# Channel statistics of a layer norm moved from TensorE to VectorE, in a hybrid decoder step on one Trainium2 core

## The reference, cut to what matters

```python
def conformer_layer(x, conv_prev, g_pre, w_in, conv_w, conv_b, ln_g, ln_b, w_out, g_post):
    h = rms_norm(x, g_pre)
    a, b, z = jnp.split(h @ w_in, 3, axis=-1)
    glu = a * jax.nn.sigmoid(b)
    full = jnp.concatenate([conv_prev, glu], axis=1)
    c = depthwise_conv(full, conv_w) + conv_b              # 31 taps
    y = jax.nn.silu(layer_norm(c, ln_g, ln_b)) * jax.nn.silu(z)
    return x + rms_norm(y @ w_out, g_post), full[:, -(CONV_W - 1):]

def layer_norm(x, g, b):
    mu = jnp.mean(x, axis=-1)                              # over 1024 channels
    var = jnp.mean(jnp.square(x - mu), axis=-1)
    return (x - mu) * lax.rsqrt(var + EPS) * g + b

def compress(rows, pe, w1, w2):                            # once for k, once for v
    # rows in chunks of 16, two chunks beside each other, against w1 (2048 x 256)
    return jax.nn.silu(pre) @ w2
```

## Time and profile before

| | |
|---|---|
| median of 3 runs | 974.96 us (973.85 to 976.8) |
| profiled execution, its own time | 973.55 us |
| its span | 971.4 us |
| PE busy | 908.4 us, 94% of the span |
| DVE, ACT, POOL busy | 530.2, 437.2, 301.2 us |

### The profile page before, as it was taken

How to read it: one execution, slowest core, us unless ns; L and a number is a source line. 1 busy time by engine, 2 the same in 40 slices (tenths; PEclk the granted TensorE clock), 3 DMA queues, 4 the chain that set the end, 5 groups by cost and what they waited for, 6 DMA issues and landing times.

```text
span 971.4 us, 16757 instructions
## 1 busy us (share of the span) xinstructions
PE 908.4 (94%) x6278; PEld 771.1 (79%) x6278; DVE 530.2 (55%) x1173; ACT 437.2 (45%) x895; POOL 301.2 (31%) x311
## 2 busy tenths in 40 slices
PE   2799999998999999999979999999999999799995
PEld 2699999954369877878979898989898988686663
DVE  2477999983861664331234555545454545535563
ACT  4356767632511533232344555455464545423421
POOL 1269888870670000003003322323232333400000
PEclk9999999999999999999979999999999999999997
DMA  7345433147618124265222222223132100922521
GB/s 215 84 111 174 119 89 96 58 111 255 220 41 296 44 82 133 49 141 155 68 70 62 66 45 66 51 60 88 36 75 44 45 1 25 271 88 82 182 78 33
DMA packets 156071, 97.43 MB, mean 100 GB/s; under 512 B 97156, under 2 KB 144932, under 8 KB 155911
## 3 DMA queue, kind: packets, MB, share of 16 engines
q1 hardware_dynamic: 141134, 77.07, 29.8%
q0 software_dynamic: 4896, 10.32, 3.1%
q10 hardware_dynamic: 9961, 8.97, 2.8%
HBM read 87.48 MB, written 18.85 MB: 109 GB/s over the span
## 4 chain that ended last, share of the span: by engine, by line
PE 84%; SPq 4%; DVE 3%; ACT 3%; DMA 3%; issue 2%; ACTq 0%; POOL 0%; DVEq 0%
PE psum L1741 9%; PE psum L2056 7%; PE psum L1760 6%; PE psum L1761 6%; PE psum L1762 6%; PE psum L2057 6%; PE psum L2058 6%; PE psum L2151 5%; PE psum L2121 4%; PE psum L2086 4%; PE psum L2104 3%; PE psum L1976 3%; PE psum L1975 3%; PE psum L1977 3%; PE psum L1833 3%; SPq L551 2%
## 5 line engine op out<-in xcount | busy, mean ns | idle before, releaser
L2056 PE MATMUL psum<-u_hi,tile_hi 128*128 128x288 f32 x464 | 147.2, 317 | 8.6 <-ACT arena L761 8.4
L761 ACT ACTIVATE arena<-psum 128x512 f32<-128x512 f32 (+9 forms) x214 | 82.1, 433 | 148.4 <-PE psum L1977 48.8
L740 POOL TENSOR_SCALAR arena<-arena,kept 128x512 f32<-128x512 f32 (+3 forms) x128 | 82.7, 661 | 184.0 <-DVE kept L1607 184.0
L2057 PE MATMUL psum<-u_lo,tile_hi 128*128 128x288 f32 x464 | 138.5, 299 | 0.0
L2058 PE MATMUL psum<-u_hi,tile_lo 128*128 128x288 f32 x464 | 137.5, 296 | 0.0
L1316 DVE SCALAR_TENSOR_TENSOR psum<-arena,psum 128x512 f32<-128x512 f32 x168 | 127.0, 756 | 6.0
L1760 PE MATMUL psum<-h_hi,tile_hi 128*128 128x288 f32 x384 | 115.2, 300 | 4.1 <-DVE tile_lo L1288 4.1
L1761 PE MATMUL psum<-h_lo,tile_hi 128*128 128x288 f32 x384 | 114.7, 299 | 0.0
L1762 PE MATMUL psum<-h_hi,tile_lo 128*128 128x288 f32 x384 | 114.3, 298 | 0.0
L2056 PEld LDWEIGHTS psum<-u_hi,tile_hi 128*128 128x128 f32 x464 | 88.3, 190 | 20.3 <-ACT arena L761 12.2
L1538 DVE COPY arena<-psum 128x512 f32<-128x512 f32 (+3 forms) x72 | 37.0, 513 | 103.8 <-PE psum L2104 101.0
(11 more groups left out here) (285 smaller groups left out, 1781.9 us busy)
## 6 DMA issues: line engine op xcount, KB each, us to landing
tile_whole<-in_b_w_in SPq DMA_DIRECT2D x64, 256.0 KB
tile_whole<-in_a_w_in SPq DMA_DIRECT2D x24, 512.0 KB
arena<-in_cmp_w SPq DMA_DIRECT2D x3, 2048.0 KB, 10.3
kvw_whole<-in_w_kv SPq DMA_DIRECT2D x6, 1024.0 KB, 11.5
bias_copies<-bias_line POOLq DMA_DIRECT2D x4, 1280.0 KB, 24.3
arena<-in_x_prompt SPq DMA_DIRECT2D x8, 512.0 KB, 10.0
arena<-in_a_w_out SPq DMA_DIRECT2D x4, 1024.0 KB, 16.8
arena<-bias_copies SPq DMA_DIRECT2D x16, 256.0 KB, 3.7
```

Of the source, the lines that this page charges most:

```text
L740: pool.tensor_scalar(L, L, rden[:, stat(n) + k:stat(n) + k + 1], gR[:, i, h:h + 1], ALU.mult, ALU.mult).then_inc(S["pn_ready"], 1)
L761: return nc.scalar.activation(out, in_, ACT.Copy, scale=scale)
L2056: pe.matmul(pb(7, HT), w_hi, u_hi[:, k, here], start=(k == 0), stop=False)
L2057: pe.matmul(pb(7, HT), w_hi, u_lo[:, k, here], start=False, stop=False)
```

## The change

The channel sums of the mean become seven adds on DVE into `chan_sum`, and one matmul of it. The squares are summed by seven adds on DVE into `square_slot(0)` (four slots in place of two, so that ACT may run ahead), and their one matmul stands between the two halves of `compress(1)`. The transposes for `conv_prompt` come ahead of `compress(0)`. The values' compression weights go into a place of their own, `w1_far`, over the prompt's GLU rows, issued ahead of chunks 25 to 27; the later reload of `w1_sb` with the same weights (needed by the prompt's compression) and `gpost_a` come behind `compress(1)`. POOL's two DRAM-to-DRAM copies come behind the bias tables. DVE's sample sums are spread anew: 0 and 1 ahead of the mean, 2 behind the copies, 3 to 6 behind the adds of squares, 7 to 9 behind the scaling, 10 to 15 last.

```diff
+        def square_slot(m):
+            i = m if m < 4 else (1, 2, 3, 1)[m - 4]
+            return sg[:, i, 0:SEQ] if i < 2 else square_far[:, i % 2]
+        SUMS = CONV * KD + KD - 1
...
@@ sync, c == C_OA, behind past_cmp(12..15)
-                if c == C_KV - 1:
-                    sp.wait_ge(S["cs_mm"], 2)
-                    sp.dma_start(w1_sb, I["cmp_w1"][1]...).then_inc(S["w1_in"], 16)
                     sp.wait_ge(S["conv_step"], CONV * KD)
                     sp.wait_ge(S["co_tr"], 1)
-                    sp.dma_start(gpost_a, ...).then_inc(S["gpost_in"], 16)
+                    sp.dma_start(w1_far, I["cmp_w1"][1]...).then_inc(S["w1_in"], 16)
+                if c == C_KV - 1:
                     for t in range(4):
...
+                    sp.wait_ge(S["stat_mm"], 1 + KD)
                     sp.dma_start(x_sb[0:NS, 4], ...).then_inc(x_in[4], 16)
+                    sp.wait_ge(S["cs_mm"], 5)
+                    sp.dma_start(gpost_a, ...).then_inc(S["gpost_in"], 16)
+                    sp.dma_start(w1_sb, I["cmp_w1"][1]...).then_inc(S["w1_in"], 16)
                     sp.wait_ge(S["sample_sums"], 2 * KD)
@@ gpsimd: L687 and L688 moved from ahead of the sample products to behind L704
@@ scalar
-                if m >= 2:
-                    act.wait_ge(S["stat_mm"], m)
-                nc.scalar.activation(sg[:, m % 2, 0:SEQ], conv[:, m, 0:SEQ], ACT.Square)
+                if m >= 4:
+                    act.wait_ge(S["conv_step"], SUMS + m - 3)
+                nc.scalar.activation(square_slot(m), conv[:, m, 0:SEQ], ACT.Square)
@@ vector
+            for m in range(1, KD):
+                dve.wait_ge(S["conv_step"], CONV * KD + m - 1)
+                V.tensor_tensor(out=chan_sum, in0=chan_sum if m > 1 else conv[:, 0, 0:SEQ], in1=conv[:, m, 0:SEQ],
+                                op=ALU.add).then_inc(S["conv_step"], 1)
+            for n in range(2):
+                sample_sum(n)
             dve.wait_ge(S["stat_mm"], 1)
...
-            for n in range(4):
+            sample_sum(2)
+            for m in range(1, KD):
+                dve.wait_ge(S["sqd"], m + 1)
+                if m > 1:
+                    dve.wait_ge(S["conv_step"], SUMS + m - 1)
+                V.tensor_tensor(out=square_slot(0), in0=square_slot(0), in1=square_slot(m), op=ALU.add)...
+            for n in range(3, 7):
                 sample_sum(n)
@@ tensor
                 for ht in range(2):
+                    if c and ht:
+                        pe.wait_ge(S["conv_step"], SUMS + KD - 1)
+                        pe.matmul(pb(1, SEQ), ones, square_slot(0), ...).then_inc(S["stat_mm"], KD)
...
-            for m in range(KD - 2):
-                mean_part(m)
-            compress(0)
-            mean_part(KD - 2)
-            mean_part(KD - 1).then_inc(S["stat_mm"], 1)
             (transposes for conv_prompt, co_tr)
+            compress(0)
+            pe.wait_ge(S["conv_step"], SUMS)
+            pe.matmul(pb(0, SEQ), ones, chan_sum, ...).then_inc(S["stat_mm"], 1)
...
-            for m in range(KD):
-                pe.wait_ge(S["sqd"], m + 1)
-                pe.matmul(pb(1, SEQ), ones, sg[:, m % 2, 0:SEQ], ...).then_inc(S["stat_mm"], 1)
             compress(1)
```

More of the change, by code:

```diff
@@ L135, in build @@
         tap_sum = at(R_X + KD * NT, SEQ)
+        chan_sum = at(R_X + KD * NT, SEQ)
+        square_far = at(R_X + 4 * D, 2, SEQ)
         last_rows_in = at(R_X + 2 * D, 4, KV, P)
@@ L167, in build @@
         w1_sb = at(R_G + 4224, 16, 256)
+        w1_far = at(R_F, 16, 256)
         rows_ring = at(R_G + 8320, 2, KV, P)
@@ L572, in _ @@
                         past_cmp(n)
-                if c == C_KV - 1:
-                    sp.wait_ge(S["cs_mm"], 2)
-                    sp.dma_start(w1_sb, I["cmp_w1"][1].rearrange("(j p) n -> p j n", p=P)).then_inc(S["w1_in"], 16)
                     sp.wait_ge(S["conv_step"], CONV * KD)
                     sp.wait_ge(S["co_tr"], 1)
-                    sp.dma_start(gpost_a, I["a_norm_post"][0:1, :].broadcast_to([P, D])).then_inc(S["gpost_in"], 16)
+                    sp.dma_start(w1_far, I["cmp_w1"][1].rearrange("(j p) n -> p j n", p=P)).then_inc(S["w1_in"], 16)
+                if c == C_KV - 1:
                     for t in range(4):
@@ L582, in _ @@
                         sp.dma_start(x_sb[:, t], I["x_prompt"][0, t * P:(t + 1) * P, :]).then_inc(x_in[t], 16)
+                    sp.wait_ge(S["stat_mm"], 1 + KD)
                     sp.dma_start(x_sb[0:NS, 4], I["x_sample"].rearrange("b t d -> (b t) d")).then_inc(x_in[4], 16)
+                    sp.wait_ge(S["cs_mm"], 5)
+                    sp.dma_start(gpost_a, I["a_norm_post"][0:1, :].broadcast_to([P, D])).then_inc(S["gpost_in"], 16)
+                    sp.dma_start(w1_sb, I["cmp_w1"][1].rearrange("(j p) n -> p j n", p=P)).then_inc(S["w1_in"], 16)
                     sp.wait_ge(S["sample_sums"], 2 * KD)
@@ L685, in _ @@
                     split_lo_a(3 * m + 7)
-            pool.dma_start(O["conv_sample"][0, :, 0:W - 1 - DS, :], I["state_conv"][0, :, DS:W - 1, :]).then_inc(S["late"], 16)
-            pool.dma_start(O["win_sample"][:, 0:PAST], I["state_win"]).then_inc(S["late"], 16)
             pool.wait_ge(S["state_ready"], 16)
@@ L704, in _ @@
                 pool.dma_start(bias_copies[h0:h0 + 4], bias_dram[h0:h0 + 4].unsqueeze(1).broadcast_to([4, P, NX])).then_inc(S["bias_out"], 16)
+            pool.dma_start(O["conv_sample"][0, :, 0:W - 1 - DS, :], I["state_conv"][0, :, DS:W - 1, :]).then_inc(S["late"], 16)
+            pool.dma_start(O["win_sample"][:, 0:PAST], I["state_win"]).then_inc(S["late"], 16)
             pool.wait_ge(S["x1_out"], 16 * TT)
@@ L904, in _ @@
                 act.wait_ge(S["centred"], m + 1)
-                if m >= 2:
-                    act.wait_ge(S["stat_mm"], m)
-                nc.scalar.activation(sg[:, m % 2, 0:SEQ], conv[:, m, 0:SEQ], ACT.Square).then_inc(S["sqd"], 1)
+                if m >= 4:
+                    act.wait_ge(S["conv_step"], SUMS + m - 3)
+                nc.scalar.activation(square_slot(m), conv[:, m, 0:SEQ], ACT.Square).then_inc(S["sqd"], 1)
             act.wait_ge(S["co_tr"], 1)
@@ L1326, in sample_sum @@
                                 ALU.add).then_inc(S["sample_sums"], 1)
+            for m in range(1, KD):
[4 more added lines that the diff above has]
+                sample_sum(n)
             dve.wait_ge(S["stat_mm"], 1)
             for m in range(KD):
-                dve.wait_ge(S["conv_step"], CONV * (m + 1))
                 V.tensor_tensor(out=conv[:, m, 0:SEQ], in0=conv[:, m, 0:SEQ], in1=pb(0, SEQ), op=ALU.subtract).then_inc(S["centred"], 1)
@@ L1335, in _ @@
                               pb(ct_bank(DB + b), KV, 16, 8)).then_inc(S["ct_ready"], 1)
-            for n in range(4):
+            sample_sum(2)
[3 more added lines that the diff above has]
+                    dve.wait_ge(S["conv_step"], SUMS + m - 1)
+                V.tensor_tensor(out=square_slot(0), in0=square_slot(0), in1=square_slot(m), op=ALU.add).then_inc(S["conv_step"], 1)
+            for n in range(3, 7):
                 sample_sum(n)
@@ L1345, in _ @@
                 V.tensor_tensor(out=conv[:, m, 0:SEQ], in0=conv[:, m, 0:SEQ], in1=rstd_ln[:, 0:SEQ], op=ALU.mult).then_inc(S["lnx_ready"], 1)
-            for n in range(4, 7):
+            for n in range(7, 10):
                 sample_sum(n)
@@ L1354, in _ @@
                 V.tensor_copy(new_rows[:, :, DS * b:DS * b + DS], glu_s[:, :, b, W - 1:W - 1 + DS]).then_inc(S["new_packed"], 1)
-            for n in range(7, 2 * KD):
+            for n in range(10, 2 * KD):
                 sample_sum(n)
@@ L1831, in compress @@
                 for ht in range(2):
+                    if c and ht:
+                        pe.wait_ge(S["conv_step"], SUMS + KD - 1)
+                        pe.matmul(pb(1, SEQ), ones, square_slot(0), start=True, stop=True).then_inc(S["stat_mm"], KD)
                     for j in range(16):
-                        ins = pe.matmul(pb(cs_bank(c, ht), 33, NCS), w1_sb[:, j, ht * P:(ht + 1) * P],
+                        ins = pe.matmul(pb(cs_bank(c, ht), 33, NCS), (w1_far if c else w1_sb)[:, j, ht * P:(ht + 1) * P],
                                         ctS[:, j % 8, :, j // 8:j // 8 + NCS], start=(j == 0), stop=(j == 15))
@@ L1864, in _ @@
             pe.wait_ge(S["glu_ready"], 3 * KD)
-            def mean_part(m):
-                pe.wait_ge(S["conv_step"], CONV * (m + 1))
-                return pe.matmul(pb(0, SEQ), ones, conv[:, m, 0:SEQ], start=(m == 0), stop=(m == KD - 1))
-            for m in range(KD - 2):
-                mean_part(m)
-            compress(0)
-            mean_part(KD - 2)
-            mean_part(KD - 1).then_inc(S["stat_mm"], 1)
             pe.wait_ge(S["sg_ready"], KD)
@@ L1878, in _ @@
             ins.then_inc(S["co_tr"], 1)
+            compress(0)
+            pe.wait_ge(S["conv_step"], SUMS)
```

(6 more changed lines are left out.)

## The result

The changed kernel takes 966.04 us (median of 4 runs, 965.39 to 968.51) against 975.62 us (4 runs) of the kernel before: ratio 0.9908, 95% interval 0.9884 to 0.9932, that is 6.6 to 11.3 us faster. Six more runs on another occasion gave 968.07 us (964.74 to 968.67), ratio 0.9924 (0.9904 to 0.9943). I had forecast 968.7, in a range of 965 to 972.5. The profiled execution took 965.92 us with a span of 964.0; against 973.55 and 971.4 that is 7.6 and 7.4 us less, where the sum said 6.3.

What follows compares the result with a forecast made beforehand. PE was taken to bound the kernel (84% of the chain), with DVE's chain then setting its restart: -8.8 us plus 2.5 us for the clock gives -6.3, from 974.96 to 968.7 us, range 965 to 972.5.

Steps and rivals of the forecast that it cites:

- the sum: Whole kernel: -8.8 us from leg 2 plus 2.5 us for the clock, together -6.3 us.
- Leg 1: PE up to compress(1): compress(0) starts at 198.25, compress(1) at 236.5 in place of 250.95, 14.5 us earlier, weights in time.
- Leg 2: DVE's chain from sum of squares to packed rows: PE idles 4.7 us, transposes start at 273.6 for 282.36, -8.8 us.
- The clock: Row products after PE's idle before the new rows' transposes: slow restart at half clock, 2.5 to 4.1 us, 2.5 taken.
- POOL against the adds: DVE beside POOL's products: L1351 kept at 8.8 us; about 2 us per blocked add could hit the new adds.
- rival 3: POOL blocks DVE's adds before eps, so DVE's chain starts 2.6 us later: 971.3 us, up to 972.9; chance 0.15.
- Moved transfers: Loads and copies issued later: gpost_a covered by 11 us, key/value weights landed at 307 before ACT reads at 332.
- case 1: The main forecast, with two clock prices and 1 us either way of DVE's chain: 967.0 to 971.3 us; chance 0.5.
- Rival 5: Queues fill with moved copies and bias tables, key/value weights land at 341, ACT 9 us late: 978 us; chance 0.05.

Runs made afterwards that it cites:

- sums-later run: Sample sums 7 to 9 moved behind the packing of the new rows, against the changed kernel: 959.86 us, ratio 0.9851 to the kernel before.
- the four corners with the squares: Changed kernel, squares on DVE or PE, sums 7 to 9 in place or behind packing: DVE 966.04 and 959.86 us, PE 965.00 and 964.56.
- the fill: Five extra 512-column matmuls, results unused, in PE's idle stretch before the new rows' transposes, against the changed kernel: 965.56 us.
- weights_late: Changed kernel, but w1_far loaded behind the output projection's weights and the first compression, copies still moved: 966.69 us, ratio 0.9917 to the kernel before.

## Why the prediction was right, point by point

- **Leg 1, PE up to the second compression: right.** 198.23 and 236.87 came out where 198.25 and 236.5 were said, with no wait for weights.
- **Leg 2, DVE's chain sets the restart: right, and shown** by the sums-later run and by the four corners with the squares. Transposes at 273.83 for 273.6, an idle of 4.65 for 4.7. What the prediction didn't draw from it is that with this chain the squares' move buys nothing.
- **The clock: right in kind, too dear.** I took 2.5 us from the two later restarts; the fill shows 1.4. The slow stretch ran from the restart at 273.83 to before 277, shorter than the 4.9 us of the earlier trace rows from which the term came. That is 1.1 of the 1.3 us by which the sum fell short of the profiled execution. The medians' further 2 us lie within their spread, in which the sparse transposes' clock has a part.
- **POOL against the adds:** the conflict is there, smaller than rival 3 had it. The squares' adds took 7.22 for 5.1 (product 5 over their start), and DVE still idled 1.80 before eps. The channel adds too took 5.91 for 5.1, with POOL's first products over their start, and were covered. L1372 stayed at 8.79 as said, and fell to 4.90 without POOL.
- **"Moved transfers": the step that failed**, though the total doesn't show it. I treated the copies' move only as a risk for what comes later, and held the early weights for safe "with POOL's copies still in the queues", 6.4 us early. The runs say the reverse: with the copies moved the weights' order matters nothing (weights_late), and the copies' place is worth 5.6 to 7.7 us, through loads that I had not looked at, the last cached rows. Beside the copies the weights would have landed at 240.7 and not at 230.1. That the forecast held is luck in this respect: the change moved the copies, so the loads landed in 3.0 us at most, and the weights in 8.4. The row that would have told it was in the trace before, 22.7 us at most against a median of 2.5.
- **A slip in the range.** With a clock price of 2.5 us at least and 1 us either way, case 1 begins at 967.7 and not at 967.0; nothing hangs on it.
- **Rival 5 (late key/value weights): absent.** Issued at 282.62, they landed in 23.2 us by the median of the two; the copies took 43.7 and nobody waited for them.

So the gain was an interplay. The squares' move is worth nothing here, and the mean's, with the transposes', 5 to 7 us. With the copies left in their old place the whole of it, mean and squares and early weights, comes out at 973.70, which can't be told from the kernel before.

## What to carry to other kernels

When work leaves the bounding engine, ask what was covered by it: a chain on another engine may now release it, and then the next microsecond is found there (here three short sums in a place where they cost 3.4 us and drew a conflict of 3.9). For everything that the bounding engine will now ask for earlier, read the *longest* landing, not the median, and what shared the queues with it. Undo each part alone, and in pairs: two of these parts made no difference when undone alone, and undoing one pair made the kernel slower than the one before.

## What the runs showed of the hardware

- A 64 KB load that usually landed in 2.4 us took up to 22.7 beside a DRAM-to-DRAM copy of some 4 MB from POOL's queue, and 3.0 at most with the copy moved; 2 MB of weights took 26.2 beside it, and 8.4 (8.2 in the run with the weights late) without.
- The granted clock fell to 0.50 behind a stretch in which PE was busy for 3.56 of 7 us, in transposes with waits of at most 1.2 us, and stayed at 1.00 in another execution with the same 3.56. Runs of one kernel lie 4 to 6 us apart in places (971.55 to 976.21, 958.26 to 964.3); one such fall cost 0.8 to 3.1 us.
- DVE instructions with two SBUF inputs took longer where they met a POOL product: eight took 8.8 us beside POOL and 4.9 without. Sample sums, with one input, took 1.16 us with POOL idle and 1.19 beside it. POOL's product was longer too (2.54 us in place of 2.13, over the adds of squares).
